# A hybrid decoder layer: the inverse's blocks moved by three whole transposes, key decays on ScalarE, z projected one turn earlier, and the fill of the turns spread anew

## The reference, cut to what matters

```python
h = rmsnorm(x, attn_norm); proj = h @ w_in
qa, ka, va, qb, kb, vb, zb, bb, ab, gl = split(proj)
oa = diff_attention(qa, ka, va)          # 8 heads, two softmaxes each, w = p0 - lam*p1
qb, kb, vb = silu(causal_dwconv(...))    # width 4
# gated delta rule: per chunk of 64 rows solve (I + tril(beta*K K^T * decay)) u = rhs
decay = exp(g[i] - g[j])  for j <= i     # g: running sums of log gates
ob = gated_delta_rule(qb, kb, vb, g, beta)       # scan over 8 chunks, state 128x128
ob = rmsnorm(ob, onorm_b) * silu(zb)
x = x + (sig(g0)*(oa@w_br_a) + sig(g1)*(ob@w_br_b)) @ w_out
x = x + (silu(conv(h@w_up)) gated) @ w_down      # D_FF 2816
x = x + sigmoid(h@w_ple_gate) * (p@w_ple_proj)
```

## Time and profile before

| | |
|---|---|
| median of 3 runs | 1238.6 us (1237.54 to 1241.13) |
| profiled execution, its own time | 1241.61 us |
| its span, first to last instruction | 1239.8 us |
| PE busy | 1153.6 us (93%) |
| DVE, ACT, POOL busy | 662.9, 509.2, 620.3 us |
| chain that ended last | PE 75%, DVE 16%, ACT 5% |

### The profile page before, as it was taken

How to read it: one execution, slowest core, us unless ns; L and a number is a source line. 1 busy time by engine, 2 the same in 40 slices (tenths; PEclk the granted TensorE clock), 3 DMA queues, 4 the chain that set the end, 5 groups by cost and what they waited for, 6 DMA issues and landing times.

```text
span 1239.8 us, 16629 instructions
## 1 busy us (share of the span) xinstructions
PE 1153.6 (93%) x5502; PEld 909.3 (73%) x5502; DVE 662.9 (53%) x1061; ACT 509.2 (41%) x798; POOL 620.3 (50%) x767
## 2 busy tenths in 40 slices
PE   6995679999898989888999999999999999999998
PEld 5783456666676766656887888888888888888886
DVE  4789876464736465465412233446776622751534
ACT  4442334445545454445233322354444422441642
POOL 6464205344434544342664564456666664574552
PEclk9997879999999999999999999999999999999999
DMA  7353003213041321321233252233433342332223
GB/s 227 86 123 90 1 13 100 77 35 94 18 108 31 84 61 34 94 68 34 69 93 94 83 171 85 85 86 102 119 86 101 92 125 72 102 98 85 69 84 90
DMA packets 196618, 104.35 MB, mean 84 GB/s; under 512 B 3926, under 2 KB 195401, under 8 KB 196553
## 3 DMA queue, kind: packets, MB, share of 16 engines
q1 hardware_dynamic: 196172, 103.39, 29.8%
q10 hardware_dynamic: 381, 0.15, 0.0%
HBM read 101.40 MB, written 2.13 MB: 84 GB/s over the span
## 4 chain that ended last, share of the span: by engine, by line
PE 75%; DVE 16%; ACT 5%; issue 3%; ACTq 0%; DVEq 0%
PE bank L524 64%; DVE pr L1542 2%; PE bank L664 1%; DVE pr L1541 1%; PE bank L625 1%; ACT pr L1077 1%; DVE dec L1587 1%; DVE o_b L1556 1%; DVE qb L1556 1%; DVE xs L1639 1%; PE bank L650 1%; DVE vb L1556 1%; DVE prod L1637 1%; PE bank L657 1%; DVE ast L1530 1%
## 5 line engine op out<-in xcount | busy, mean ns | idle before, releaser
L460 POOL TENSOR_TENSOR w_lo<-w_raw,w_hi 128x256 fp32r<-128x256 f32 x692 | 541.8, 817 | 259.7 <-ACT w_hi L1005 253.9
L524 PE MATMUL bank<-hn_hi,w_hi 128*128 128x512 f32 x1000 | 421.7, 422 | 1.0 <-DVE o_a L1815 1.0
L524 PE MATMUL bank<-hn_hi,w_lo 128*128 128x512 f32 x1000 | 395.4, 395 | 0.0
L524 PE MATMUL bank<-hn_lo,w_hi 128*128 128x512 f32 x1000 | 394.9, 395 | 0.0
L475 POOL CAST w_hi<-w_raw 128x1024 fp32r<-128x1024 f32 x70 | 75.2, 1074 | 343.0 <-PE bank L524 263.6
L524 PEld LDWEIGHTS bank<-hn_hi,w_hi 128*128 128x128 f32 x1000 | 191.0, 191 | 49.0 <-issue 15.2
L524 PEld LDWEIGHTS bank<-hn_hi,w_lo 128*128 128x128 f32 x1000 | 190.7, 191 | 42.1
L524 PEld LDWEIGHTS bank<-hn_lo,w_hi 128*128 128x128 f32 x1000 | 191.3, 191 | 38.2 <-issue 5.7
L1005 ACT ACTIVATE w_hi<-w_raw 128x1024 fp32r<-128x1024 f32 x111 | 117.9, 1063 | 77.4 <-PE bank L524 69.8
L1928 DVE SCALAR_TENSOR_TENSOR u<-vr,pt,u 128x511 f32<-128x511 f32 x88 | 89.3, 1015 | 8.0 <-DVE u L1928 0.2
L1922 DVE TENSOR_TENSOR vr<-bank,rs 128x512 f32<-128x512 f32 x44 | 30.4, 692 | 72.9 <-PE bank L524 67.5
(11 more groups left out here) (280 smaller groups left out, 1647.1 us busy)
## 6 DMA issues: line engine op xcount, KB each, us to landing
w_raw<-in_w_in SPq DMA_DIRECT2D x73, 512.0 KB, 6.5
w_raw<-in_w_up SPq DMA_DIRECT2D x44, 512.0 KB, 3.8
w_raw<-in_w_down SPq DMA_DIRECT2D x16, 512.0 KB, 3.9
crow<-cum_rows_out SPq DMA_DIRECT2D x16, 256.0 KB, 5.6
w_raw<-in_w_br_a SPq DMA_DIRECT2D x8, 512.0 KB, 3.9
w_raw<-in_w_br_b SPq DMA_DIRECT2D x8, 512.0 KB, 3.9
w_raw<-in_w_out SPq DMA_DIRECT2D x8, 512.0 KB, 4.0
w_raw<-in_w_ple_gate SPq DMA_DIRECT2D x8, 512.0 KB, 4.1
```

The lines of the kernel that those rows point to most:

```text
L460: ins = pool.tensor_tensor(wlo[c.slot][:, ks, :], raw[c.slot][:, ks, :], whi[c.slot][:, ks, :].bitcast(F32), ALU.subtract)
L524: mm = pe.matmul(acc, w[c.slot][:, i, :], xx[:, x0 + i, :], start=(i == 0 and n == 0), stop=last)
```

## The change

What it does:

- DVE's four strip transposes of the gather become one of 128 partitions. For that, blocks 1 and 3 are first copied beside the others by two ACT copies per head (`diagonals`). The seven strip transposes back become two of 128 partitions (`turn_back`), into `dd` and `li`; PE's `pair_low` and `pair_high` read those directly, and `xf` is filled by four ACT copies (`place_rows`, `place_columns`) and two POOL copies. `half_low` and `half_high` wait for the ACT ones.
- `key_decay` moves from DVE to ACT: four 128x128 Relu with the running sum as bias, then exp with scale -1.
- TURN's order is qb, vb, qa, ka, va, zb; zb is projected one turn ahead, so the lead turn has six chunks, not five, and the last turn has nine, not ten, since one chunk of the mix moves into turn 6. `gate_z(h)` on ACT moves from the late part of turn h to just behind `keep_w(a, 0)`.
- In the turns, `qk_sum(h+2, 0)` goes ahead of `turn_w(a, 3)` and `qk_sum(h+2, 1)` into the scan; the steps are spread anew. In the lead turn, the attention of head 0 is finished (`attend`, both `qk_sum`) ahead of `pair_low`, DVE's pieces of `substitute` are cut anew, and `prep(0, 0)` stands ahead of the gather.

```diff
-STEPS = ((2, 3, 2, 3, 3, 1, 3, 3, 1, 5), ((1, 1), (1, 1, 1), (1, 1, 1), (1, 1, 1)), (3, 3))
-STEPS_LATE = ((3, 3, 1, 3, 3, 1, 2, 2, 1, 3), ((1, 0), (1, 1, 1), (1, 1, 1), (1, 1, 1)), (0, 0))
-STEPS_LAST = ((2, 3, 2, 3, 4, 1, 3, 3, 1, 3), ((1, 1), (2, 2, 2), (2, 2, 2), (2, 2, 2)), (0, 0))
+STEPS = ((2, 3, 1, 3, 5, 1, 3, 5, 1, 4, 5), ((1, 1), (1, 1, 1), (1, 1, 1), (1, 1, 1)))
+STEPS_LATE = ((2, 3, 1, 2, 4, 1, 2, 3, 1, 2, 2), ((0, 0), (1, 1, 1), (1, 1, 1), (1, 1, 1)))
+STEPS_LAST = ((2, 3, 2, 3, 4, 1, 3, 3, 1, 2, 1), ((1, 1), (2, 2, 2), (2, 2, 2), (2, 2, 2)))
...
-TURN = ("qb", "vb", "zb", "qa", "ka", "va")
-LEAD = ("qb", "vb", "qa", "ka", "va")
-LATE = ("qb", "vb", "zb", "zl")
+TURN = ("qb", "vb", "qa", "ka", "va", "zb")
+LATE = ("qb", "vb", "zb")
...
             for h in range(H - 2):
                 for n in range(len(TURN)):
                     both(stream.heads[h].at(n))
+                    if h == 0 and n == 0:
+                        pool.wait_ge(sem("turned_back"), 2)
+                        pool.wait_ge(low_ready, stream.heads[0].at(0).number + 1)
+                        for b in range(2):
+                            pool.tensor_copy(xf[strip(b), :, strip(b)], li[strip(b), :, :]).then_inc(sem("xf_set"), 1)
...
             for h in range(H):
                 f.step(2)
                 key_products(h)
-                f.step(6)
-            qk_sum(0, 0, stream.first.at(0))
+                f.step(3)
+                if h == H - 1:
+                    qk_sum(0, 0, stream.first.at(0))
+                f.step(3)
+            f.step(3)
+            qk_sum(0, 1, stream.first.at(1))
             f.rest()
-            qk_sum(0, 1, stream.first.at(1))
...
             def pair_low(g):
-                pe.wait_ge(sem("blocks"), 1)
+                pe.wait_ge(sem("turned_back"), 1)
...
             def half_low(g):
+                pe.wait_ge(sem("placed"), 2)
...
                 f.step(before[9])
+                if more_a:
+                    qk_sum(h + 2, 0, at("qa"))
+                f.step(before[10])
                 if attention:
                     turn_w(a, 3)
...
+                    if t == 1 and more_a:
+                        qk_sum(h + 2, 1, at("ka"))
                     if t == 2 and attention:
                         attention_sum(a)
-                for n, name in enumerate(("qa", "ka")):
-                    f.step(late[n])
-                    if more_a:
-                        qk_sum(h + 2, n, at(name))
                 if attention:
                     f.rest()
...
-            def key_decay_exp(h):
-                act.wait_ge(sem("key_rows_read"), h + 1)
-                done(nc.scalar.activation(decs[h % 2][:, :, :], decs[h % 2][:, :, :], ACT.Exp), "key_dec", h + 1)
+            def key_decay(h):
+                act.wait_ge(sem(f"key_rows{h % 2}"), 16 * (h // 2 + 1))
+                if h > 1:
+                    act.wait_ge(sem("lower"), h - 1)
+                for t in range(NT):
+                    ins = nc.scalar.activation(decs[h % 2][:, t, :], crows[h % 2][:, t, :], ACT.Relu,
+                                               bias=gates[:, G_CUM, t, h:h + 1], scale=-1.0)
+                done(ins, "key_rows_read", h + 1)
+                done(nc.scalar.activation(decs[h % 2][:, :, :], decs[h % 2][:, :, :], ACT.Exp, scale=-1.0), "key_dec", h + 1)
+            def diagonals(h):
+                m = slice(h * NT, (h + 1) * NT)
+                act.wait_ge(sem("lower"), h + 1)
+                nc.scalar.activation(dd[strip(1), m, 0:SUB], dd[strip(1), m, SUB:2 * SUB], ACT.Copy)
+                done(nc.scalar.activation(dd[strip(3), m, 0:SUB], dd[strip(3), m, SUB:2 * SUB], ACT.Copy), "diagonals", h + 1)
...
             def gather():
-                for b in range(4):
-                    at = SUB * (b % 2)
-                    ins = V.transpose(li[strip(b), :, :], dd[strip(b), :, at:at + SUB].rearrange("p n i -> p i n"))
-                link(ins)
+                dve.wait_ge(sem("diagonals"), H)
+                link(V.transpose(li[:, :, :], dd[:, :, 0:SUB].rearrange("p n i -> p i n")))
...
+            def turn_back():
+                dve.wait_ge(sem("xf_set"), 1)
+                done(V.transpose(dd[:, :, 0:SUB].rearrange("p n c -> p c n"), xs[:, :, :].rearrange("p i c -> p c i")),
+                     "turned_back", 1)
+                done(V.transpose(li[:, :, :].rearrange("p n i -> p i n"), xs[:, :, :]), "turned_back", 2)
...
-                    side = [lambda: decay(a)] + finish_silu(a, 2)
+                    side = finish_silu(a, 2) + [lambda: decay(a)]
+                if more_a:
+                    side.append(lambda: prep(h + 2, 0))
```

More of the change, by code:

```diff
@@ L746, in lead_turn @@
                 turn_w(0, 1)
+                f.step(1)
+                scores(0, 2)
+                f.step(8)
+                turn_w(0, 2)
+                f.step(1)
+                scores(0, 3)
+                k_turn(0)
+                f.step(4)
+                qk_sum(1, 0, at("qa"))
+                f.step(4)
+                turn_w(0, 3)
+                v_turn(0)
                 f.step(2)
-                scores(0, 2)
-                f.step(6)
-                turn_w(0, 2)
+                attend(0)
                 f.step(2)
-                scores(0, 3)
-                f.step(4)
-                k_turn(0)
+                attention_sum(0)
+                qk_sum(1, 1, at("ka"))
+                f.step(1)
                 pair_low(0)
@@ L783, in turn @@
                 f = Fill(*fill)
-                before, scan, late = steps
+                before, scan = steps
                 if attention:
@@ L1229, in lead_turn, with turn @@
                 decay_exp(0)
[L1230 to L1233 removed]
+            def turn(h, at, gate_at, attention=True, more_a=True):
                 a = h + 1
@@ L1246, in turn @@
                     keep_w(a, 0)
+                gate_z(h, gate_at("zb"))
+                if attention:
                     first_tap(a, 0, at("qb"))
@@ L1308, in _ @@
                 silu_exp(h, 1)
+                if h > 1:
+                    diagonals(h - 2)
                 if h > 0:
-                    key_decay_exp(h - 1)
+                    key_decay(h - 1)
+            diagonals(H - 2)
+            key_decay(H - 1)
             prep_qk(0, 0, stream.first.at(0))
-            key_decay_exp(H - 1)
+            diagonals(H - 1)
+            prep_r(0, 0, stream.first.at(0))
             prep_qk(0, 1, stream.first.at(1))
-            prep_r(0, 0, stream.first.at(0))
             key_norms()
+            prep_r(0, 1, stream.first.at(1))
             prep_v(0, stream.first.at(2))
-            prep_r(0, 1, stream.first.at(1))
-            lead_turn(place(stream.lead, LEAD))
+            places = [place(stream.lead, TURN)] + [place(stream.heads[h], TURN) for h in range(H - 2)] + [place(stream.late, LATE)]
+            lead_turn(places[0])
             for h in range(H - 2):
-                turn(h, place(stream.heads[h], TURN))
-            turn(H - 2, place(stream.late, LATE), more_a=False)
-            turn(H - 1, place(stream.late, LATE), attention=False, more_a=False)
+                turn(h, places[h + 1], places[h])
+            turn(H - 2, places[H - 1], places[H - 2], more_a=False)
+            turn(H - 1, None, places[H - 1], attention=False, more_a=False)
             ob_r(H - 1)
@@ L1762, in turn @@
                 if attention:
-                    side = [lambda: decay(a)] + finish_silu(a, 2)
+                    side = finish_silu(a, 2) + [lambda: decay(a)]
+                else:
+                    side = [lambda: None] + [lambda q=q: mix_a(q, stream.mix_a.at(2 + q), sqr[q]) for q in range(2)]
+                if more_a:
+                    side.append(lambda: prep(h + 2, 0))
                 dve.wait_ge(sem("v_mm"), h * NT + 1)
@@ L1793, in turn @@
                                             op0=ALU.mult, op1=ALU.add), "ob_mixed", h + 1)
-                if more_a:
-                    prep(h + 2, 1)
-                if not attention:
-                    mix_a(0, stream.mix_a.at(2), sqr[0])
-                    mix_a(1, stream.mix_a.at(3), sqr[1])
             def finish_z(h):
@@ L1838, in _ @@
             LINKS = {}
-            lead_turn(place(stream.lead, LEAD))
+            lead_turn(place(stream.lead, TURN))
             for h in range(H - 2):
```

180 lines of the change are left out of this document (82 added, 98 removed).

## The result

The kernel after takes 1201.58 us (median of 4 runs, 1200.42 to 1202.43); before, in 4 runs beside it, 1239.87 us. The ratio is 0.969, 95% interval 0.967 to 0.971. The forecast was 1191, range 1177 to 1214: the direction is right, the size 10.6 us short. The profiled execution took 1202.43 us; its span, from the first to the last instruction, is 1200.7 us, for 1239.8 before.

What follows compares the result with a forecast made beforehand. PE's work bounds it from 620 us, DVE the lead turn, PE's waits add in the turns. Savings 16.3 + 28.0 + 1.4 + 1.3 + 5.4 = 52.4 us gave 1186 by the median; with 5 us reserve 1191, range 1177 to 1214.

Steps and rivals of the forecast that it cites:

- Key phase: Key heads: ACT sets the pace with the decays, 7.4 us a head for 6.46, silu 7 ending at 91.5.
- Gather: Lead turn: one whole transpose takes 2.0 us for 8.05 in strips; first scores at 110.4, 2.3 us earlier.
- Substitution: Lead turn on DVE, from ka ready to the first transpose back: 44.1 us for 45.3, ending at 154.5.
- Inverse to turn 0: From pair_low to turn 0: 23.1 us for 29.85, since PE's attention work goes ahead; turn 0 at 179.8.
- Turns 0 to 5: Six middle turns: k-steps and sums moved ahead cover PE's waits, saving 28.0 us.
- Turns 6 and 7: Last turns: shorter chain 1.4, earlier gate_z 1.3 and one chunk less 5.4 us saved.
- Reserve: Whole kernel: 5 us left in the forecast total for small new waits.
- Whole transposes cost four strips: Rival, lead turn: each of the three whole transposes takes about 8 us, total 1205; chance 0.06.
- covers that fail: Rival, turns: each turn keeps about half its waits, 14 us less saved, about 1203; chance 0.2.
- ACT pays the 512-column price: Rival: every small ACT activation costs as much as 512 columns, key phase 13 us longer, 1204; chance 0.05.
- The edit of the lead turn pays nothing: Rival: DVE's cuts miss PE's deliveries and the longer key phase eats the gather; only turns' 36 us remain, 1205; chance 0.06.
- Denser PE loses its clock in the turns: Rival, turns: PE without pauses is granted less clock, slower than before, about 1250 at 0.85; chance 0.03.

Runs made afterwards that it cites:

- warm_after: Kernel after plus fifteen 128x512 PE products that nobody reads, ahead of pair_low and both half_low blocks: 1191.71 us, ratio 0.964.
- covers_back: Kernel after with the first nine fill counts of turns 0 to 5 as before and the second sum one scan piece later: 1218.83 us.
- strips: Kernel after with each of the three whole transposes done as four of 32 partitions: 1217.52 us, ratio 0.982.
- decays_and_attend: Kernel after with key decay exponents back on DVE and attend(0) with its sum back among the blocks: 1189.10 us.
- four_edits: Kernel after with key decays on DVE, attend(0) and its sum among the blocks, decay first in turn 6, prep(0,0) behind the gather: 1185.28 us.
- attend_among_blocks: Kernel after with attend(0) and its sum put back between pair_high and half_high on PE: 1196.60 us, ratio 0.965.
- key_decays_on_dve: Kernel after with the exponents of the key decays made on DVE as before, diagonals' copies left on ACT: 1191.14 us, ratio 0.961.

## Why the prediction was right in sign and short in size

By the spans the forecast was 52.4 us saved, 47.4 with its reserve, and 39.1 came. That the total lies in the stated range is in part luck: the lead turn and turns 6 and 7 fell 20.9 us short, and turns 0 to 5 gave 7.6 more than forecast, by busy time that the prediction did not count. The steps, as the prediction put them:

- **Key phase** (head 7.4 us, silu 7 at 91.5): it came at 94.99. The mechanism was right, ACT sets the pace, and the named bound contains the value; the mis-sized term is "back to back they overlap, so I take 0.22 each". The records of the Relu are

```profile
L1195 ACT ACTIVATE dec<-crow,gates x32: 385/387/407, 47.9 to 100.6; 128x128 f32<-128x128 f32 x32
```

so one takes 0.39 us and not the interpolated 0.32. In a row of four they do overlap, by 0.1 us each as the prediction had it: the row takes 1.28 us, for 0.9. The two copies take 0.31 us each and don't overlap (87.06 and 87.38), 0.63 for 0.5. Head 7.97 us, 3.5 us in all. That the edit is a loss by itself was forecast; the run prices it at 8.7 us at turn 0.
- **Gather** (starts at 101.4, first scores at 110.4): 2.0 us for a whole transpose is exact. From silu 7's end to the gather 12.2 us passed for 9.9, and from there to the scores 12.0 for 9.0, since POOL's splitting met the four first rows of the substitution, which took 5.5 us and not 2.2. "May cost 1 to 2 us" was 3.
- **Substitution** (44.1 us): 41.3. PE's deliveries were there; 2.8 us better than forecast.
- **Inverse to turn 0** (23.1 us): 30.7 in the kernel after. This is the step that failed. The prediction took the granted clock as given here; its only look at the clock was for the turns. With `attend` and the sums moved out, PE did 18.4 us of the stretch at 0.50. With the clock held the stretch takes 22.7 us (warm_after). That this meets the 23.1 is luck in part: the 29.85 us that the prediction subtracts from hold 8.7 us at 0.50, which it did not read, so its sum was not one at full clock; at full clock the busy time of that piece alone would be some 4 us less (an estimate, half of 8.70). Together with the three steps above that is 16.3 us forecast and 2.7 measured. The experiments price what stands against each other at turn 0: whole transposes 15.8 gained (10 without their effect on the clock), the low clock 8.1 lost, the decays 8.7 lost. They share the clock, so they don't add up.
- **Turns 0 to 5** (28.0 us): 35.6. PE's idle time went as forecast, 28.1 us before (336.4 less 308.3 busy), 1.1 after; the cover theory is shown by covers_back for the waits at i = 1 and 2, not for i = 3. Not counted were 8.6 us of busy time (308.3 to 299.7): before, three of the six turns ran at 0.97 and took 56.6 to 56.9 us for 55.3, and a turn at 1.00 keeps PE busy 50.7 us there, as in covers_back, for 50.0 after. This extra gain is luck.
- **Turns 6 and 7** (8.1 us): 0.8. The chunk saved is real, 5.4 us between `ob_sum` and the mix (52.5 us for 57.9), but turn 6 took 52.2 us for 50.0 (clock, and the state's wait behind the decay, a term that the prediction did not have), and turn 7 39.2 for 36.9, with a wait of 1.6 us for `oa_lo`, which its fill now asks for eight steps sooner.
- **Reserve** (5 us): the sum fell 13.3 us short, more than twice the reserve.
- **Rivals.** "Whole transposes cost four strips" and "covers that fail" are refuted. "ACT pays the 512-column price" is refuted at 0.32 us. "The edit of the lead turn pays nothing" came out nearly so (2.7 us), for one of its two reasons, the longer key phase, and one that it did not name, the clock. "Denser PE loses its clock in the turns" was the wrong way about: the dense turns 0 to 5 run at 1.00, and it was the stretch of small products and short waits that lost it.

## What to carry to other kernels

Moving large products out of a stretch of many small ones can cost more than it saves: look at the granted clock of the stretch before and after, and price its remaining work at both levels. A cover is worth at least the wait it hides: taking two steps away brought back 0.57 and 1.08 us, the numbers of before. Before work goes to an engine that is idle half of the time, look at what its idle time is. In the key phase before, ACT was busy for only 14.62 of 31 us, but most of the rest was the 2.56 us a head in which it stands for `conv`, which itself waits for ACT's tap. The new instructions stand ahead of the next tap and not in that gap: it is 2.56 us after the change as well. A head got 1.9 us of ACT's work more and 1.51 us longer (7.97 for 6.46), as a wait of 0.49 us for DVE's decays went. Whether the Relu would be free inside the gap was not tried.

## What the runs showed of the hardware

- A PE that the records show busy for 18.40 of 18.40 us was granted 0.50, with 96 products of 64x64 and five k-steps in it, behind two runs of 128 products of 32x32 and waits of 1.79 and 0.95 us; fifteen 128x512 products added ahead of those runs and behind them kept it at 1.00. The same work mixed evenly was granted 0.50 from 164 to 195 us. The same 422 products in the same order, without a wait, were granted 0.78 in decays_and_attend and 0.88 in four_edits. Three kernels with the same turn 6 (after, attend_among_blocks, key_decays_on_dve) were granted 0.89, 0.96 and 1.00 over its first 46 us.
- STREAM_TRANSPOSE of 128 partitions by 1024 elements takes 2.0 to 2.2 us, the same of 32 partitions 1.9 to 2.2 (8.72 us for four in `strips`).
- A 128x128 Relu with a bias, out of SBUF, takes 0.39 us, and in a row of four the next starts 0.30 us after it; a copy of 32x128 takes 0.31, and the next starts 0.32 after it.
- DVE's four decays took 4.00 us at 165.49 and 2.94 in turn 6, while POOL copied, cast or split, for 1.14 alone. The Trainium skill ("SBUF — State Buffer", section "Who interferes with whom") has DVE and GpSimd take turns at one shared pair of ports; the trace agrees in kind.
